# Two plain iterations instead of three in the convolved gate stages, with two activation sums made by GpSimd

## The reference, cut to what matters

```python
def conv_ffn(h, w_gate, w_up, conv_w, conv_b, w_down):
    g = causal_dwconv(h @ w_gate, conv_w, conv_b)      # 3 taps along the tokens, per feature
    return (jax.nn.silu(g) * (h @ w_up)) @ w_down
```

## Time and profile before

| | us |
|---|---|
| median of 3 runs | 2388.21 |
| lowest and highest | 2386.76, 2393.13 |
| the profiled execution | 2386.84 |
| its span, first to last instruction | 2385.0 |
| PE busy | 2340.6 (98%) |
| DVE busy | 1587.9 (67%) |
| ACT busy | 1029.4 (43%) |
| POOL busy | 339.0 (14%) |

### The profile page before, as it was taken

One profiled execution on the slowest core, in us unless ns is written; L12 is line 12 of the kernel. 1 busy time (PEld: TensorE's weight loads), 2 busy tenths in 40 slices (PEclk: granted clock), 3 DMA queues, 4 the chain that ended last, 5 costly groups with the idle time before them and its releaser, 6 DMA issues.

```text
span 2385.0 us, 36878 instructions
## 1 busy us (share of the span) xinstructions
PE 2340.6 (98%) x14899; PEld 2037.7 (85%) x14899; DVE 1587.9 (67%) x2174; ACT 1029.4 (43%) x1352; POOL 339.0 (14%) x294
## 2 busy tenths in 40 slices
PE   7699999999999999999999999999999999999999
PEld 7688899988886678999878779999888877899987
DVE  8845877846536777777585546899534545799942
ACT  6421544532225725445234444556423344455622
POOL 6402000002002240000224241000121002000000
PEclk9899999999999999999999999999999999999999
DMA  2422333233232122332333313233332212333332
GB/s 58 104 97 90 105 107 105 83 101 113 89 99 69 40 94 85 107 103 82 96 107 110 89 64 114 82 105 89 101 102 85 93 66 71 89 107 107 85 107 85
DMA packets 328844, 219.67 MB, mean 92 GB/s; under 512 B 11188, under 2 KB 319050, under 8 KB 328618
## 3 DMA queue, kind: packets, MB, share of 16 engines
q1 hardware_dynamic: 322298, 208.46, 29.6%
q0 software_dynamic: 3024, 7.90, 1.4%
q10 hardware_dynamic: 3360, 1.02, 0.2%
HBM read 206.59 MB, written 2.10 MB: 87 GB/s over the span
## 4 chain that ended last, share of the span: by engine, by line
PE 90%; DVE 4%; POOL 3%; ACT 2%; issue 1%; SPq 0%; DMA 0%; DVEq 0%; ACTq 0%; POOLq 0%
PE psum L1380 9%; PE psum L1382 9%; PE psum L1381 9%; PE psum L1136 9%; PE psum L1138 9%; PE psum L1137 9%; PE psum L1349 3%; PE psum L1350 3%; PE psum L1351 3%; PE psum L1524 2%; PE psum L1525 2%; PE psum L1526 2%; PE psum L1248 1%; PE psum L1244 1%; PE psum L1245 1%; PE psum L1228 1%
## 5 line engine op out<-in xcount | busy, mean ns | idle before, releaser
L2093 ACT CAST w_hi<-w_stage 128x2048 fp32r<-128x2048 f32 x129 | 246.7, 1912 | 691.8 <-PE psum L1138 408.4
L2973 DVE TENSOR_TENSOR w_lo<-w_stage,w_hi 128x2048 fp32r<-128x2048 f32 x126 | 300.0, 2381 | 275.6 <-ACT w_hi L2093 275.6
L1380 PE MATMUL psum<-x_sum_hi,w_hi 128*128 128x256 f32 x1088 | 308.0, 283 | 0.2 <-issue 0.2
L1382 PE MATMUL psum<-x_sum_hi,w_lo 128*128 128x256 f32 x1088 | 307.9, 283 | 0.0
L1381 PE MATMUL psum<-x_sum_lo,w_hi 128*128 128x256 f32 x1088 | 307.9, 283 | 0.0
L2163 ACT CAST w_hi<-w_parts 128x1024 fp32r<-128x1024 f32 x204 | 213.3, 1049 | 200.9 <-PE psum L1382 111.1
L3101 DVE TENSOR_TENSOR w_lo<-w_parts,w_hi 128x1024 fp32r<-128x1024 f32 x204 | 248.1, 1219 | 51.7 <-ACT w_hi L2163 50.5
L1380 PE MATMUL psum<-x_hi,w_hi 128*128 128x256 f32 x816 | 230.9, 283 | 0.0
L1381 PE MATMUL psum<-x_lo,w_hi 128*128 128x256 f32 x816 | 230.9, 283 | 0.0
L1382 PE MATMUL psum<-x_hi,w_lo 128*128 128x256 f32 x816 | 230.9, 283 | 0.0
L1136 PE MATMUL psum<-hidden_raw_hi,w_hi 128*128 128x512 f32 x572 | 223.6, 391 | 0.3 <-DVE w_lo L2973 0.3
(11 more groups left out here) (584 smaller groups left out, 5283.5 us busy)
## 6 DMA issues: line engine op xcount, KB each, us to landing
w_stage<-in_ffn_w_down_dram SPq DMA_DIRECT2D x64, 704.0 KB, 4.6
w_parts<-in_ffn_w_gu_dram SPq DMA_DIRECT2D x144, 256.0 KB, 3.4
w_parts<-in_ffn_w_gate_dram SPq DMA_DIRECT2D x64, 256.0 KB, 3.1
w_parts<-in_ffn_w_up_dram SPq DMA_DIRECT2D x64, 256.0 KB, 3.1
w_stage<-in_sb_w_qkv_dram SPq DMA_DIRECT2D x12, 1024.0 KB, 5.1
w_stage<-in_od_w_in_dram SPq DMA_DIRECT2D x12, 1024.0 KB, 5.2
w_stage<-in_ev_w_in_dram SPq DMA_DIRECT2D x10, 1024.0 KB, 5.0
w_stage<-in_ssm_w_glu_dram SPq DMA_DIRECT2D x8, 1024.0 KB, 5.5
```

Of the source, the lines that this page charges most:

```text
L1380: nc.tensor.matmul(dst, hi, x_hi[:, k, :], start=(start and k == 0), stop=False, skip_group_check=True)
L1382: mm = nc.tensor.matmul(dst, lo, x_hi[:, k, :], start=False, stop=(k == DC // 2 - 1), skip_group_check=True)
L2093: nc.scalar.copy(whi[:, half, :], wst[:, half, :]).then_inc(whi_done, 1)
L2973: V.tensor_tensor(wlo[:, half, :], wst[:, half, :], whi[:, half, :].bitcast(F32), ALU.subtract).then_inc(wlo_done, 1)
```

## The change

1. `SEVEN` of conv0 and conv1 goes from 3 to 2: the third plain iteration becomes a ninth seven-product iteration.
2. The seven early steps are taken from DVE and given to POOL, with the same operations on the same data, behind `square_sums(5)` for conv0 and behind `square_sums(7)` for conv1. They wait for the whole norm (`x_ready`) and count on a new semaphore `x_parts`. ACT's rounding of `x_sum[2]` and `x_sum[3]` and DVE's step 4 wait for it.
3. DVE keeps five steps, all behind the last split of plain weights. ACT's order of the rounds stays 2, 3, 0, then the gates, then 1.
4. The PSUM bank that an iteration uses (`x_bank`) is now counted from the last iteration backwards, so that the last one uses the same bank as before. In gu0 and gu1 this gives the same banks as before.

```diff
-SEVEN = {"gu0": 2, "gu1": 2, "conv0": 3, "conv1": 3}
+SEVEN = {"gu0": 2, "gu1": 2, "conv0": 2, "conv1": 2}
-X_STEPS = {"gu0": 4, "gu1": 4, "conv0": 12, "conv1": 12}
+X_STEPS = {"gu0": 4, "gu1": 4, "conv0": 5, "conv1": 5}
+X_PARTS = {"gu0": 0, "gu1": 0, "conv0": 7, "conv1": 7}
...
-        def x_bank(tile, i):
-            return bank[4 + 2 * tile + i % 2]
+        def x_bank(name, tile, i):
+            return bank[4 + 2 * tile + (SEVEN_ITERS[name] - 1 - i + (name in ("conv0", "conv1"))) % 2]
...
+            def x_step(name, n, ins):
+                ins.then_inc(x_parts, 1)
+                pool.wait_ge(x_parts, parts_count(name, n))
+
+            def later_block_sums(name, n):
+                pool.wait_ge(x_ready, x_count(n + 1))
+                rows = slice(0, DC // 2), slice(DC // 2, DC)
+                (b11, c11), (b12, c12), (b21, c21), (b22, c22) = (
+                    [x[:, rows[m], TOKEN_HALVES[h]].bitcast(F32) for x in (xhi, xlo)] for m in range(2) for h in range(2))
+                third, fourth = x_sum[2][:, :, :], x_sum[3][:, :, :]
+                x_step(name, 1, nc.gpsimd.tensor_tensor(third, b22, b12, ALU.subtract))
+                x_step(name, 2, nc.gpsimd.tensor_tensor(third, third, c22, ALU.add))
+                x_step(name, 3, nc.gpsimd.tensor_tensor(third, third, c12, ALU.subtract))
+                x_step(name, 4, nc.gpsimd.tensor_tensor(fourth, third, b11, ALU.add))
+                x_step(name, 5, nc.gpsimd.tensor_tensor(fourth, fourth, c11, ALU.add))
+                x_step(name, 6, nc.gpsimd.tensor_tensor(fourth, fourth, b21, ALU.subtract))
+                x_step(name, 7, nc.gpsimd.tensor_tensor(fourth, fourth, c21, ALU.subtract))
...
             square_sums(5)
+            later_block_sums("conv0", 5)
             square_sums(6)
...
             square_sums(7)
+            later_block_sums("conv1", 7)
...
                 if conv:
-                    for n, made in ((2, 3), (3, 7), (0, 10)):
-                        round_sum(n, made)
-                    plain_gates(plain - 1, lambda: round_sum(1, 12))
+                    round_sum(2, 3, x_parts)
+                    round_sum(3, 7, x_parts)
+                    round_sum(0, 3)
+                    plain_gates(plain - 1, lambda: round_sum(1, 5))
...
-                def x_sums_from_parts_early():
+                def x_sums_from_parts():
                     dve.wait_ge(x_ready, x_count(norm_in + 1))
-                    b11, b21 = high_low(first, 0), high_low(second, 0)
-                    difference(1, x_sum[2][:, :, :], high_low(second, 1), high_low(first, 1))
-                    step(4, V.tensor_tensor(x_sum[3][:, :, :], x_sum[2][:, :, :], b11[0], ALU.add))
...
                     dve.wait_ge(wlo_done, (st.it0 + plain) * 2)
                     b11 = high_low(first, 0)
-                    difference(8, x_sum[0][:, :, :], b11, high_low(first, 1))
-                    step(11, V.scalar_tensor_tensor(x_sum[1][:, :, :], x_sum[2][:, :, :], -1.0, b11[0], ALU.mult, ALU.subtract))
-                    step(12, V.tensor_tensor(x_sum[1][:, :, :], x_sum[1][:, :, :], b11[1], ALU.subtract))
+                    difference(1, x_sum[0][:, :, :], b11, high_low(first, 1))
+                    dve.wait_ge(x_parts, parts_count(name, 3))
+                    step(4, V.scalar_tensor_tensor(x_sum[1][:, :, :], x_sum[2][:, :, :], -1.0, b11[0], ALU.mult, ALU.subtract))
+                    step(5, V.tensor_tensor(x_sum[1][:, :, :], x_sum[1][:, :, :], b11[1], ALU.subtract))
...
                     plain_iteration(0)
-                    x_sums_from_parts_early()
-                    plain_iteration(1)
-                    x_sums_from_parts_late()
+                    x_sums_from_parts()
                     x_sum_low(0, 3)
                     for u in range(2):
-                        taps(4 + u, u, bank[u])
+                        taps(2 + u, u, bank[u])
```

More of the change, by code:

```diff
@@ L425, in build_blocks @@
         product_done, copied, added, x_low = sem("product_done"), sem("copied"), sem("added"), sem("x_low")
+        x_parts = sem("x_parts")
         block = ctx.enter_context(nc.Block())
@@ L527, in summed_count, with parts_count @@
             return steps + (before(name) + i) * 6 + n
+        def parts_count(name, n):
+            return sum(X_PARTS[other] for other in list(SEVEN)[:list(SEVEN).index(name)]) + n
         def copied_count(name, i, n):
@@ L1391, in seven_products @@
                 for i in range(SEVEN_ITERS[name]):
-                    x_of = [x_bank(tile, i)[:, 0:HALF] for tile in range(2)]
+                    x_of = [x_bank(name, tile, i)[:, 0:HALF] for tile in range(2)]
                     for tile in range(2):
@@ L2142, in plain_gates, with round_sum @@
                             nc.scalar.activation(tmp_a[:, u, :], tmp_a[:, u, :], ACT.Silu).then_inc(act_out, 1)
-                def round_sum(n, made):
-                    act.wait_ge(summed, summed_count(name, 0, made - X_STEPS[name]))
+                def round_sum(n, made, by=summed):
+                    if by is x_parts:
+                        act.wait_ge(x_parts, parts_count(name, made))
+                    else:
+                        act.wait_ge(summed, summed_count(name, 0, -X_STEPS[name]) + made)
                     nc.scalar.copy(x_sum_hi[n][:, :, :], x_sum[n][:, :, :]).then_inc(rounded, 1)
@@ L2184, in fork @@
                         act.wait_ge(evac_done, hidden_count(name, i - 1, 1))
-                    nc.scalar.copy(y_half(tile), x_bank(tile, i)[:, 0:HALF]).then_inc(copied, 1)
+                    nc.scalar.copy(y_half(tile), x_bank(name, tile, i)[:, 0:HALF]).then_inc(copied, 1)
                 def gate_first(i):
@@ L2204, in gate_second @@
                     if conv:
-                        nc.scalar.activation(tmp_a[:, 1, :], x_bank(0, i), ACT.Copy, scale=tap(layer, TAPS - 1, m)).then_inc(conv_a, 1)
+                        nc.scalar.activation(tmp_a[:, 1, :], x_bank(name, 0, i), ACT.Copy, scale=tap(layer, TAPS - 1, m)).then_inc(conv_a, 1)
                     else:
-                        nc.scalar.activation(tmp_a[:, 1, :], x_bank(0, i), ACT.Silu, scale=-1.0).then_inc(act_out, 1)
+                        nc.scalar.activation(tmp_a[:, 1, :], x_bank(name, 0, i), ACT.Silu, scale=-1.0).then_inc(act_out, 1)
                 def silu_first(i):
@@ L3113, in seed @@
                     dve.wait_ge(copied, copied_count(name, i, 2 * tile + 1))
-                    V.tensor_tensor(w_half(tile), x_bank(tile, i)[:, 0:HALF], z_kept[:, tile, :], ALU.add).then_inc(added, 1)
+                    V.tensor_tensor(w_half(tile), x_bank(name, tile, i)[:, 0:HALF], z_kept[:, tile, :], ALU.add).then_inc(added, 1)
                 def join(i, tile):
-                    x = x_bank(tile, i)
+                    x = x_bank(name, tile, i)
                     dve.wait_ge(product_done, products_count(name, i, 9 + 2 * tile))
@@ L3124, in taps_second @@
                 def taps_second(i):
-                    taps(2 * (plain + i) + 1, 1, x_bank(0, i))
+                    taps(2 * (plain + i) + 1, 1, x_bank(name, 0, i))
                 def hidden_first(i):
@@ L3135, in hidden_second @@
                     dve.wait_ge(act_out, gated_count(name, i, 2))
-                    V.scalar_tensor_tensor(hraw[:, 2 * (plain + i) + 1, :], x_bank(1, i), -1.0, tmp_a[:, 1, :],
+                    V.scalar_tensor_tensor(hraw[:, 2 * (plain + i) + 1, :], x_bank(name, 1, i), -1.0, tmp_a[:, 1, :],
                                            ALU.mult, ALU.mult).then_inc(evac_done, 1)
@@ L3190, in conv_start @@
                     low_pair(0, 0, 0)
-                    plain_hidden(2, 0)
+                    plain_hidden(1, 0)
                     low_pair(0, 0, 1)
@@ L3194, in conv_start @@
                         sum_of_three(0, tile)
-                    plain_hidden(2, 1)
+                    plain_hidden(1, 1)
                     low_pair(0, 1, 0)
```

4 lines of the change are left out of this document (removed).

## The result

| | before | after |
|---|---|---|
| median of 15 runs, us | 2387.44 | 2393.29 |
| lowest and highest | 2386.39, 2393.13 | 2392.28, 2397.02 |
| ratio, 95% interval | | 1.0023 [1.0015, 1.0031] |
| the profiled execution | 2386.84 | 2392.47 |
| its span | 2385.0 | 2390.7 |

The change makes the kernel slower by 5.9 us (0.23%), which is less than 0.3% but clear of zero. I had forecast 2392.0 us, 5.0 us above the profiled execution of before.

The account below looks back on a forecast made before the run. The prediction took PE's matmul issue as the bound, with no waits in the convolved gate stages. Its terms, -3.2 + 7.0 + 1.2 = +5.0 us, gave 2391.8 from 2386.84; it named 2392.0, range 2385.5 to 2396.5 (8 in 10).

Parts of the forecast that it names:

- The exchanged iteration: conv0 and conv1: a seven-product iteration lasts 20.16 us, the plain one it replaces 21.76; -1.60 per stage, -3.2 in all.
- POOL alone is in time: Before the seven-product part: POOL's seven passes, undisturbed, would end at 1476.0, in time for DVE's step 4 and ACT's rounding.
- The lateness d: End of DVE's five x-sum steps: POOL and DVE hold each other up, ending at 1486.03 instead of 1482.3; 3.7 us late.
- The stops: Start of the seven-product part: PE stands about 2.2 us at the first product, 1 more at the ninth; two stages +7.0.
- the slower first matmuls: PE's first matmuls after a stop run slower: 0.2 us added per stage, within the 3.5.
- The end of the stage: Start of the down stage: ring half 0 stays in use until the twelfth product; 0.58 us per stage, two stages +1.2.
- Rival 3: End of the stage: the weight ring costs nothing or more, 0 to 1.4 us per stage; inside the range, no separate chance.
- The literal sum by the Trainium skill: DVE against POOL: the second instruction takes its whole time after the first; d = 4.1, total 0.8 us above the forecast.
- Rival 1: Start of the seven-product part: POOL's passes fit beside DVE, PE never stops; -2.0 us, 2384.8; chance 0.23.
- Rival 2: POOL's pass 7 starved, ACT's order binding: d = 6.0, 5.6 us of stop each, +9.2, 2396.0; chance 0.13 with slower passes.
- the releaser that the profile would name: PE's first product: the profile would show DVE `hidden_raw` L3030 as releaser of the 2 us stop.
- The upper bound: Whole kernel, with d at its largest, 6.0, and 5.6 us of stop per stage: 2396.1 us, elsewhere 2396.0.

Follow-up runs that it names:

- g_gaps: Changed kernel with f_ring's edit; early steps in DVE's gaps, only step 3 on POOL, during DVE's taps: 2383.9 us, again 2384.67.
- a_three_plain: Changed kernel with three plain iterations as before, POOL still making the seven early steps: 2387.37 us, ratio to before 1.000.
- c_pool_four: Changed kernel with POOL's passes 5 to 7 left out, so the fourth sum lacks three terms: 2385.78 us, 0.9995 to before.
- d_memsets: Changed kernel with POOL's passes 6 and 7 replaced by five memsets of the same size: 2385.7 us, 0.9994 to before.
- b_all_dve: Changed kernel with all twelve x-sum steps on DVE behind the last split, none on POOL: 2404.98 us, 1.0075 to before.
- e_copies: d_memsets with five copies of the third sum into the fourth in place of the memsets: 2392.68 us, one run only.
- f_ring: Changed kernel; ACT's first down-stage cast no longer waits for ring slots the down weights don't cover: 2391.96 us, 1.0017 to before.

## Why the prediction was right

- **The exchanged iteration, -1.60 us per stage:** g_gaps measures 1.59 and 1.60 with all waits gone.
- **POOL alone is in time, and free of cost in itself:** its fourth sum ends at 1480.8, and a_three_plain is level with before. ACT's order never held DVE.
- **The lateness d, forecast 3.7:** the fifth step ends at 1486.93, less the 0.59 by which the stage began later 1486.3, against the 1482.3 of a start without POOL: 4.0. The turns fell as forecast (pass 6, split, pass 7, first step). The 0.3 that I had too little came before them: POOL starts 0.06 later than I had it (1459.65 less 0.59), each pass takes 2.40 in place of 2.36, with 0.08 between, and so pass 6 begins 0.28 later (1474.00 less 0.59, against 1473.13) and holds more of the split.
- **The stops, forecast 2.2 and 1, 3.5 with the slower first matmuls:** the first product comes 2.6 us after where the plain iteration ends (1472.07 + 21.79 = 1493.86), the ninth another 1.0 (12.51 behind the first in place of 11.51). From the stretch: 2.60 + 1.60 - 0.58 = 3.6. That forecast and stretch agree to 0.1 is in part luck. The 0.2 for slower first matmuls had no row behind it, and no run shows it at this size. In the profile of after, only three matmuls of each stage follow after 0.19 to 0.20 in place of 0.12, two of them ahead of the ninth product's wait, which takes them up; what the lateness alone gives, 4.0 - 0.55 + 0.11, is already 3.6. So d was 0.3 too small and this term nearly as much too large.
- **The end of the stage, 0.58 per stage:** in the profile of after the down stage's first matmul has the 0.35 us stop of gu0 in both stages. c_pool_four and d_memsets, without stops at the start, stand at -1.02 = -1.60 + 0.58. Rival 3, a ring that costs 0 to 1.4 per stage, is this same term.
- **The literal sum by the Trainium skill** (SBUF — State Buffer, section Who interferes with whom: the second instruction takes its whole time, +0.8 us in all) was an estimate of d = 4.1, the trace has 4.0. But that is no evidence for it: the turns themselves went as the rows had them (2.15 of 2.29 and 1.08 of 1.23 after the release), and the difference to 3.7 is the later pass 6.
- **Rival 1** (POOL fits beside DVE) was ruled out by the trace and is what c_pool_four makes: 2.1 us faster in the stages, forecast 2.0. **Rival 2** (POOL starved): pass 7 got its turn between two DVE instructions that follow each other within 0.1 us.
- What I had wrong beside these sizes: the releaser that the profile would name. And my median was 1.3 us low: 0.7 are in the profiled executions (5.7 against 5.0), of these 0.6 before the stage; the rest, the median 0.8 above its own profiled execution, isn't explained by any run. The lowered clock after a stop, seen in three other kernels, could add to it in some executions, but in those where I can see it 1.0 us of it went into the ninth product's wait. The upper bound, given as 2396.1 and as 2396.0, is 2396.0 by its own terms.

## What to carry to other kernels

Work given to an idle engine isn't free where that engine shares an access with the one relieved. Here a POOL pass that met DVE's work held it for 2.0 us (the first step took 3.23 in place of 1.23), longer than the 1.23 us step that it replaces; laid beside DVE instructions with an operand in PSUM it held nothing. Lateness of a helper that a stage hides behind a long independent piece of PE work comes to light when that piece is taken away: before removing an iteration, list the room of each wait behind it (here 1.55 and 0.55 us). And half-width matmuls cost more than half (0.120 against 0.227 us), so that seven products for eight save 7%, not 12.5%.

## What the runs showed of the hardware

- A POOL memset of 128 x 1024 (1.0 us each) leaves a DVE instruction with two SBUF operands alone; a copy of the same size (1.04 us alone) and a two-input pass (2.40) exclude it, and where both engines had work waiting, they took turns one by one (five copies in 10.03 us; pass 6, split, pass 7, first step).
- A stop of TensorE can cost beyond itself: granted 1.2 in place of 2.4 GHz after a stop of 7.0 us (b_all_dve, both stages, 24 and 13 matmuls 0.20 to 0.22 us apart), after one of 1.9 us (e_copies) and one of 2.4 us (f_ring, both with 16 or 17 such matmuls in each stage), but not after one of 2.4 us in the changed kernel. What decides is open. e_copies and f_ring ran on one chip and b_all_dve on another, and the chip of the changed kernel isn't on record, so that a difference between chips isn't excluded either.
